# Layer one's gate product on split operands, and eight key pages moved into the second layer's gate

## The reference

```
h = x
layer 0:  h = h + gla_mixer(rms_norm(h, g_pre[0]))            # in-projection q, k, v, g, gated linear attention, w_out
          h = h + sigmoid(rms_norm(h, g_ple[0]) @ w_ple_gate[0]) * (p[0] @ w_ple_up[0])
shared:   k, v = rms_norm(h, g_kv) @ w_kv                      # joined to the paged cache for the samples
layer 1:  h = h + sb_mixer(rms_norm(h, g_pre[1]))              # q and gate from sb_w_in, stick-breaking attention, sb_w_out
          h = h + sigmoid(rms_norm(h, g_ple[1]) @ w_ple_gate[1]) * (p[1] @ w_ple_up[1])
y = rms_norm(h, g_final)
```

## Time and profile before

| | us |
|---|---|
| median of 3 runs | 890.15 (889.59 to 891.01) |
| the profiled execution, its own time | 891.36 |
| its span in the profile | 889.6 |
| PE busy | 846.0 (95%) |
| VectorE busy | 553.7 (62%) |
| ScalarE busy | 455.4 (51%) |
| GpSimd busy | 277.4 (31%) |
| chain that ended last | PE 75%, DVE 10%, DMA 6%, ACT 5% |

### The profile page before, as it was taken

One profiled execution on the slowest core, in us unless ns is written; L12 is line 12 of the kernel. 1 busy time (PEld: TensorE's weight loads), 2 busy tenths in 40 slices (PEclk: granted clock), 3 DMA queues, 4 the chain that ended last, 5 costly groups with the idle time before them and its releaser, 6 DMA issues.

```text
span 889.6 us, 14838 instructions
## 1 busy us (share of the span) xinstructions
PE 846.0 (95%) x5063; PEld 583.9 (66%) x5063; DVE 553.7 (62%) x678; ACT 455.4 (51%) x1532; POOL 277.4 (31%) x151
## 2 busy tenths in 40 slices
PE   5999999989999999999998999999989999999995
PEld 3566677767754444444477878778744444799995
DVE  4345475788856869989996632232267777555553
ACT  4512383237658677769672412212288666444433
POOL 2000000866666998995780000000100000021110
PEclk9999999999999999999999999999999999999998
DMA  9899868646599998989995079998898879321202
GB/s 332 293 398 336 313 234 292 219 151 228 204 308 370 377 331 296 343 311 337 354 339 199 1 248 328 368 332 288 304 339 299 316 269 364 102 95 49 95 1 96
DMA packets 109435, 232.62 MB, mean 261 GB/s; under 512 B 7473, under 2 KB 66488, under 8 KB 109360
## 3 DMA queue, kind: packets, MB, share of 16 engines
q1 hardware_dynamic: 50992, 172.26, 53.2%
q10 hardware_dynamic: 58368, 59.41, 20.0%
HBM read 220.51 MB, written 11.14 MB: 260 GB/s over the span
## 4 chain that ended last, share of the span: by engine, by line
PE 75%; DVE 10%; DMA 6%; ACT 5%; issue 3%; POOL 1%; SPq 1%; ACTq 0%; POOLq 0%; DVEq 0%
PE pp L1652 20%; PE pp L1639 15%; PE pp L1655 10%; PE pp L2087 6%; PE pp L2044 4%; DVE slot L1298 3%; PE pp L2071 2%; PE pp L1616 2%; DMA w_raw<-in_gla_w_in_dram 2%; PE pp L1693 2%; PE pp L2058 2%; PE pp L1636 2%; PE pp L1667 2%; DVE w_lo L1116 1%; DMA slot<-in_cache_k_dram 1%
## 5 line engine op out<-in xcount | busy, mean ns | idle before, releaser
L629 POOL TENSOR_TENSOR slot<-slot,qb 128x1024 f32<-128x1024 f32 x95 | 247.5, 2635 | 100.6 <-DMA slot<-in_cache_k_dram 62.7
L1299 DVE TENSOR_REDUCE zall<-slot 128x16 f32<-128x1024 f32 x99 | 119.0, 1214 | 18.1 <-POOL slot L629 17.0
L1116 DVE TENSOR_TENSOR w_lo<-w_raw,w_hi 128x1024 fp32r<-128x1024 f32 x55 | 77.5, 1408 | 74.5 <-ACT w_hi L674 74.5
L829 ACT ACTIVATE slot<-slot 128x64 f32<-128x64 f32 x464 | 111.0, 241 | 21.8 <-POOL slot L629 21.8
L674 ACT CAST w_hi<-w_raw 128x1024 fp32r<-128x1024 f32 x56 | 58.5, 1045 | 71.3 <-PE pp L1655 34.2
L829 ACT ACTIVATION_READ_ACCUMULATOR slot<-slot 128x1 f32 x464 | 86.8, 187 | 0.0
L1639 PE MATMUL pp<-xn,w_raw 128*128 128x512 f32 x192 | 84.3, 593 | 0.5 <-ACT xn L685 0.5
L1639 PE MATMUL pp<-xn,w_unsplit 128*128 128x512 f32 x192 | 83.9, 592 | 0.0
L1652 PE MATMUL pp<-xb_hi,w_hi 128*128 128x260 f32 x384 | 79.2, 287 | 1.1 <-DVE w_lo L1116 0.9
L1655 PE MATMUL pp<-xa_hi,w_hi 128*128 128x512 f32 x192 | 78.6, 409 | 1.6 <-DVE w_lo L1116 1.6
L1652 PE MATMUL pp<-xb_lo,w_hi 128*128 128x260 f32 x384 | 77.3, 283 | 0.0
(11 more groups left out here) (322 smaller groups left out, 1442.2 us busy)
## 6 DMA issues: line engine op xcount, KB each, us to landing
slot<-in_cache_k_dram SPq DMA_DIRECT2D x128, 512.0 KB, 5.6
slot<-in_cache_v_dram SPq DMA_DIRECT2D x120, 512.0 KB, 5.4
w_raw<-in_gla_w_in_dram ACTq DMA_DIRECT2D x12, 1024.0 KB, 6.2
slot<-in_gla_w_in_dram SPq DMA_DIRECT2D x24, 512.0 KB, 9.5
w_raw<-in_w_kv_dram ACTq DMA_DIRECT2D x8, 1024.0 KB, 9.8
w_raw<-in_w_ple_gate_dram ACTq DMA_DIRECT2D x6, 1024.0 KB, 5.2
s<-in_state_gla_dram SPq DMA_DIRECT2D x1, 4096.0 KB, 19.9
out_dram<-s ACTq DMA_DIRECT2D x4, 1024.0 KB, 8.0
```

Of the source, the lines that this page charges most:

```text
L629: nc.gpsimd.tensor_tensor(slot[s][:], slot[s][:], qb[:, (n // NPG) % 2, :], ALU.mult).then_inc(S("k_mul_pool"), 1)
L829: ins = nc.scalar.activation(part, part, ACT.Copy, accum_out=zall[:, n % NPG, b * SH + h:b * SH + h + 1])
L1116: nc.vector.tensor_tensor(lo, raw, hi.bitcast(F32), ALU.subtract).then_inc(S("w_split"), 1)
L1299: nc.vector.tensor_reduce(zall[:, n % NPG, b * SH:(b + 1) * SH], at.rearrange("p (h d) -> p h d", d=HD), AX.X, ALU.add).then_inc(S("k_used ...
```

## The change

ple0 leaves `UNSPLIT` and becomes a split stage. Its input, set 2 of `X_SETS`, becomes a split set and moves to the B buffers, and VectorE gets an `x_lo` in each job of wo0 (after the page sums in the first six jobs, before them in the last two). The two extra weight buffers now serve only from q1 on (`WHOLE0`): wo0 and ple0 use the two raw ones. In wo0 `load_pair` stands behind ScalarE's `x_hi` of every second job and waits for the products of the pair that used the buffer before. `split_hi` and `split_lo` of ple0's first job stand in wo0's last job (in front of the residual add on VectorE), those of its further jobs at the head of the job before. `PAGES_AT` gives ple0's jobs three pages each, all multiplied by GpSimd, the first summed by ScalarE in every other job; g1's second and third job take four pages each. The turn back of the scores and the sigmoids with the scan move one job later (to g1's sixth job), the turn back of the weights to its eighth.

```diff
@@ -46,13 +46,13 @@
 NJOBS = _j
 WITH_SAMPLES = ("g1", "K", "V", "wo1", "ple1")
 
-UNSPLIT = ("wo0", "ple0", "q1", "g1")
+UNSPLIT = ("wo0", "q1", "g1")
 
 GFINAL, GOUT, BGK, NVEC = 40, 48, 50, 54
 
-X_SETS = ("A", "B", "A", "B", "B", "B", "A")
+X_SETS = ("A", "B", "B", "B", "B", "B", "A")
 X_GAIN = (0, GOUT, 16, 8, 32, None, 24)
-X_SPLIT = (0, 4, 5, 6)
+X_SPLIT = (0, 2, 4, 5, 6)
 
 
 S_STAGES = (("qk", 8), ("v", 8), ("g", 8), ("wo", 8), ("up", 2), ("ple", 8), ("q1", 8))
@@ -65,8 +65,8 @@
 
 
 PAGES_AT = {}
-for _name, _c in (("v", (0, 0, 0, 0, 1, 3, 2, 2)), ("g", (2, 3, 2, 3, 2, 3, 2, 3)), ("wo0", (4,) * 8), ("ple0", (4,) * 8),
-                  ("q1", (4,) * 8), ("g1", (4, 0, 0, 0, 0, 0, 0, 0))):
+for _name, _c in (("v", (0, 0, 0, 0, 1, 3, 2, 2)), ("g", (2, 3, 2, 3, 2, 3, 2, 3)), ("wo0", (4,) * 8), ("ple0", (3,) * 8),
+                  ("q1", (4,) * 8), ("g1", (4, 4, 4, 0, 0, 0, 0, 0))):
     for _u in range(PHASES[_name][1]):
         PAGES_AT[PHASES[_name][0] + _u] = _c[_u]
 PAGES_THROUGH = {}
@@ -93,13 +93,15 @@
 
 QUAD = 4
 
-PAIR_BUF, PAIR_TURN = {}, {}
+WHOLE0 = PHASES["q1"][0] // 2
+PAIR_BUF, PAIR_TURN, PAIR_LAST = {}, {}, {}
 for _p in range(1, NJOBS // 2):
-    _first = PHASES[UNSPLIT[0]][0] // 2
-    _native = _first <= _p < PHASES["K"][0] // 2
-    PAIR_BUF[_p] = (1, 0, 2, 3)[(_p - _first) % 4] if _native else _p % 2
-    PAIR_TURN[_p] = sum(b == PAIR_BUF[_p] for b in PAIR_BUF.values())
-assert PHASES[UNSPLIT[0]][0] // 2 % 2 == 1
+    _four = WHOLE0 <= _p < PHASES["K"][0] // 2
+    PAIR_BUF[_p] = (1, 0, 2, 3)[(_p - WHOLE0) % 4] if _four else _p % 2
+    _before = [_q for _q in range(1, _p) if PAIR_BUF[_q] == PAIR_BUF[_p]]
+    PAIR_TURN[_p] = len(_before) + 1
+    PAIR_LAST[_p] = _before[-1] if _before else None
+assert WHOLE0 % 2 == 1
 
 ZC = 3 * SH
 ZW = NPG * NS // 2 * ZC
@@ -167,8 +169,10 @@
 
 def on_act(n):
 
-    return any(len(pages_at(j)) >= 4 and n in pages_at(j)[:2 if phase_of(j) == "q1" and j % 2 == 0 else 1]
-               for j in PAGES_THROUGH)
+    for j in PAGES_THROUGH:
+        if n in pages_at(j):
+            name, of = phase_of(j), n - pages_at(j)[0]
+            return of < (2 if name == "q1" and j % 2 == 0 else j % 2 if name == "ple0" else len(pages_at(j)) >= 4)
 
 
 def summed_by_act(n):
@@ -330,7 +334,7 @@
         pT0 = at("pT0", [P, 2, NP_TOK], F32, off_small)
         oP = offA + size([P, KT, T])
         pin0 = at("pin0", [P, TB, PLE], F32, oP)
-        xn = {1: at("xn1", [P, KT, T], F32, offA), 2: at("xn2", [P, KT, T], F32, offB), 3: at("xn3", [P, KT, T], F32, oP)}
+        xn = {1: at("xn1", [P, KT, T], F32, offA), 3: at("xn3", [P, KT, T], F32, oP)}
         xb_hi, xb_lo = (at(n, [P, KT, T], F32R, offB + i * size([P, KT, T])) for i, n in enumerate(("xb_hi", "xb_lo")))
 
 
@@ -652,13 +656,14 @@
 
                 if p >= NJOBS // 2:
                     return
-                whole0 = PHASES[UNSPLIT[0]][0] // 2
-                if (unsplit(2 * p) and p >= whole0 + 4) or (p >= 2 and not unsplit(2 * p) and unsplit(2 * p - 4)):
-                    act.wait_ge(S("mm"), tiles_through(2 * (p - 4) + 1))
-                elif PAIR_BUF[p] >= 2:
-                    act.wait_ge(S("mm"), tiles_through(2 * whole0 - 1))
-                elif p >= 3:
-                    act.wait_ge(S("w_split"), splits_through(2 * (p - 2) + 1))
+                q = PAIR_LAST[p]
+                if q is None:
+                    if PAIR_BUF[p] >= 2:
+                        act.wait_ge(S("mm"), tiles_through(2 * WHOLE0 - 1))
+                elif unsplit(2 * q):
+                    act.wait_ge(S("mm"), tiles_through(2 * q + 1))
+                else:
+                    act.wait_ge(S("w_split"), splits_through(2 * q + 1))
                 dst = pair_buffer(p) if unsplit(2 * p) else raw_pair(p)
                 act.dma_start(dst, weight_pair_source(p)).then_inc(S(f"w_in{PAIR_BUF[p]}"), 16)
 
@@ -669,10 +674,11 @@
                 p = j // 2
                 act.wait_ge(S(f"w_in{PAIR_BUF[p]}"), 16 * PAIR_TURN[p])
                 if j >= 4:
-                    act.wait_ge(S("mm"), tiles_through(PHASES["K"][0] - 3 if unsplit(j - 2) else j - 2))
+                    act.wait_ge(S("mm"), tiles_through(j - 2 if not unsplit(j - 2) else
+                                                       PHASES["K"][0] - 3 if phase_of(j) == "K" else PHASES["wo0"][0] - 1))
                 raw, hi, _ = split_views(j)
                 nc.scalar.copy(hi, raw).then_inc(S("w_hi"), 1)
-                if j % 2 == 0 and j > 2 and j != PHASES["K"][0]:
+                if j % 2 == 0 and j > 2 and j not in (PHASES["K"][0], PHASES["ple0"][0]):
                     load_pair(p + 1)
 
             def x_hi(n, src):
@@ -908,17 +914,20 @@
 
             def loads_at(j):
 
-                if j == PHASES["wo0"][0]:
+                if j == PHASES["q1"][0]:
                     load_pair(j // 2 + 2)
                 if j % 2 == 0 and j // 2 + 3 <= PHASES["K"][0] // 2 + 1:
                     load_pair(j // 2 + 3)
 
             for u in range(8):
                 j = PHASES["wo0"][0] + u
-                loads_at(j)
                 sum_page(j)
+                if u == 7:
+                    split_hi(j + 1)
                 act.wait_ge(S("evac"), tiles_through(j))
                 x_hi(2 * KT + u, hT[:, u, 0:NP_TOK])
+                if u % 2:
+                    load_pair(j // 2 + 2)
                 square(KT + u, hT[:, u, 0:NP_TOK])
                 if u == 1:
                     for c in range(2):
@@ -927,7 +936,9 @@
                     rms(1)
             for u in range(8):
                 j = PHASES["ple0"][0] + u
-                loads_at(j)
+                split_hi(j + 1)
+                if u == 7:
+                    load_pair(WHOLE0 + 1)
                 sum_page(j)
                 act.wait_ge(S("evac"), tiles_through(j))
                 sigmoid_tile(8 + u, work[:, 2 + u % 2, 0:NP_TOK], work[:, 2 + u % 2, 0:NP_TOK])
@@ -1013,10 +1024,10 @@
                     if i >= 4:
                         x_hi(4 * KT + 2 * i - 8, hT[:, 2 * i - 8, :])
                         x_hi(4 * KT + 2 * i - 7, hT[:, 2 * i - 7, :])
-                    if i == 4:
+                    if i == 5:
                         for g in range(4):
                             sample_sigmoids(g)
-                    if i == 6:
+                    if i == 7:
                         for g in range(4):
                             sample_weights_out(g)
                 if 8 <= i < 23:
@@ -1408,11 +1419,17 @@
 
             for u in range(8):
                 j = PHASES["wo0"][0] + u
+                if u == 7:
+                    split_lo(j + 1)
                 add_residual(j, u)
-                if u:
+                if u < 6 and u:
+                    score_pages(j)
+                x_lo(2 * KT + u, hT[:, u, 0:NP_TOK])
+                if u >= 6:
                     score_pages(j)
             for u in range(8):
                 j = PHASES["ple0"][0] + u
+                split_lo(j + 1)
                 if u == 0:
                     recip(1)
                 add_gated(j, u, 8 + u, u + 1)
@@ -1462,7 +1479,7 @@
                     sample_rows(done)
                 if i < 8:
                     normed(j, g1T[:, u, :])
-                    if i < 3:
+                    if i < 5:
                         score_pages(j)
                     if i >= 4:
                         x_lo(4 * KT + 2 * i - 8, hT[:, 2 * i - 8, :])
@@ -1642,7 +1659,7 @@
                         last.then_inc(S("mm"), 1)
                     return
                 _, wh, wl = split_views(j)
-                for k in range(KT):
+                for k in tiles:
                     if wait_x:
                         pe.wait_ge(S("x_ready"), x_order(x0 + k) + 1)
                     xh, xl = x_parts(x0 + k)
@@ -1654,7 +1671,8 @@
                         else:
                             last = nc.tensor.matmul(bank[banks_of(j)[0]], w[:, k, :], x[:, 0:NP_TOK],
                                                     start=(k == 0 and first), stop=(k == KT - 1 and w is wl))
-                last.then_inc(S("mm"), 1)
+                if tiles[-1] == KT - 1:
+                    last.then_inc(S("mm"), 1)
 
             def up_tile0(u):
 
```

## The result

The changed kernel took 909.75 us (median of 4, 905.1 to 918.28), the kernel before 889.87 beside it: a ratio of 1.0239 (95% interval 1.0195 to 1.0283). It is slower, as forecast. The size was not: I said 904.1 with 909.0 as the upper end. The profiled execution took 905.1 (span 903.4), 13.7 more than that of before. So the forecast of the sum (+13.95) meets the profiled run, and misses the median by another 4.7.

What follows compares the result with a forecast made beforehand. TensorE, without idle time in wo0's later part and ple0, was taken as the bound. Pair 16 8.05, ple0 0.9, the clock 1.7 and g1 3.3 summed to +13.95 us on 890.15: 904.1, range 894.6 to 909.

Steps and rivals of the forecast that it cites:

- The clock: Start of ple0: one fall to half clock for 3.4 us after the wait for product 36, +1.7 us.
- the first split: End of wo0: job 34's split halves ready at 320.5 to 321.6, covered by the weights' wait, so 0.
- The gain per product: ple0: a product takes 5.68 us split, 6.87 unsplit; 9.5 us over eight, 7.1 from product 36 to q1.
- Pair 16: wo0: weights of jobs 32 and 33 land late with two buffers, at 303.9; product 32 later by 8.05 us.
- The second and third product: ple0's start: products 35 and 36 wait about 4 and 6 us for split weights; +7.5 to 8.5, middle 8.0.
- before product 35 a fall costs nothing, as the next wait absorbs it: ple0's start: a fall to half clock ahead of product 35 adds 0, hidden in the wait for product 36.
- The third rival: Whole kernel: the clock falls twice or more and g1 is at its far end of 6 us: 909; chance 0.14.
- q1: Stage q1: same pages and same products as before, so 0.
- g1: g1 to K: scan a job later, K's first product waits for its split weights; +3.3 us, ends 0 and 6.
- The sum: Whole kernel: 8.05 + 0.9 + 1.7 + 3.3 = +13.95 us, giving 904.1.

Runs made afterwards that it cites:

- second profile: The changed kernel once more, no edit, with a second trace: median 909.98 us, ratio 1.0245; the profiled run took 908.07.
- buffers only: The kernel before with only two raw weight buffers in wo0 and ple0, loads placed as in the change, ple0 unsplit: 906.07 us, ratio 1.0196.
- the last experiment: The changed kernel with the page plan of before and each pair asked for ahead of wo0's page sum: 903.87 us, ratio 1.0195.
- the fillers: Matmuls that nothing reads, put before products 32, 35 and 36 of the changed kernel: 908.02 us, ratio 1.0194.
- pages only: The kernel before with only the change's page plan and later turns and sigmoids: 895.45 us, ratio 1.0051.

## Why the prediction was right in sign and short in size

Two terms of the sum failed. The clock was put at 1.7 us with one fall, where the two profiled runs of the changed kernel show four and five falls that cost 5.4 and nearly 8. And the first split was put at nothing, hidden behind the weights' wait, where product 34 waited a further 1.81 and 3.31 us for it.

- **The gain per product** was right. Jobs 36 to 42 took 50.7 us instead of 56.8, 6.0 less; with the 1.7 us that a fall at 346 cost this is the forecast 7.1 and a little more. TensorE set ple0's period.
- **Pair 16 (+8.05)** was mis-sized and the mechanism right: the load landed in 11.9 us, the wait was 4.79 (4.41 in the second profile). The experiments add what I did not price: when the load goes out. ScalarE's program order decides it, not the product that frees the buffer. They also show that the terms don't add as my sum adds them: the late weights alone (buffers only) cost 16 us of medians, the split on top of them 1.4 more. That the sum meets one profiled run doesn't show what each term is worth by itself.
- **"The first split (hidden)"** failed. With pair 16 late, product 34 still waited 1.81 and 3.31 us for `w_lo`, and 5.52 when it was in time. I had the engines work on while TensorE waited. But ScalarE stood still for 2.66 us before a square, whose buffer TensorE frees with the square sum behind product 33; the page sums, `w_hi` and `w_lo` stand behind that (timelines of ScalarE and VectorE):

```profile
315.93 0.63 ACT L702 ACTIVATE work<-hT 128x512 f32<-128x512 f32 x1 [2.66 <-PE pp L1711]
...
320.29 1.03 ACT L680 CAST w_hi<-w_raw 128x1024 fp32r<-128x1024 f32 x1
```
```profile
321.35 1.45 DVE L1127 TENSOR_TENSOR w_lo<-w_raw,w_hi 128x1024 fp32r<-128x1024 f32 x1 [0.60 <-ACT w_hi L680]
```

So the late job 32 pushed the split back and did not hide it: `w_lo` was ready at 322.8, and I had 320.5 to 321.6. VectorE had been busy until 320.75 and would hardly have begun sooner. Its eight `x_lo` were to be 0.7 us each and to fall in its waits; one took 0.74, the others 1.43 and more beside GpSimd:

```profile
309.45 1.59 DVE L1136 SCALAR_TENSOR_TENSOR xb_lo<-hT,gcol,xb_hi 128x512 fp32r<-128x512 f32 x1
...
313.30 2.81 DVE L1136 SCALAR_TENSOR_TENSOR xb_lo<-hT,gcol,xb_hi 128x512 fp32r<-128x512 f32 x1 [1.66 <-ACT xb_hi L691]
```

- **The second and third product (+7.5 to 8.5)** came at +8.5 in the profiled run and at +11.4 in the second profile. The waits are the other way round from what I had (4 us, then 6): 5.13 and 3.09, since product 35 ran at half clock and took 2.5 us of the second wait. That term is the larger part of the split's price, as the last experiment bears out.
- **The clock (+1.7)** is the term that fell shortest. I had one fall of 3.4 us. There were four in the profiled run, 17.0 us, and 23.8 in the second profile. Three of the four slowed work that no later wait absorbs (job 32's 8.83 less 7.03 is 1.8, which job 34's wait doesn't absorb since its `w_lo` hangs on TensorE's square sums; 1.7 at 346; 1.9 behind K): 5.4 us, and not 1.7. And "before product 35 a fall costs nothing, as the next wait absorbs it" overlooked product 34: a fall there moves the square sum on which job 35's halves wait, 3 us. With it the falls of the second profile cost nearly 8 (1.8, 2.9, 1.7, and 1.3 behind K). From run to run the mean clock goes with the time: 0.985 for 905.1 us, 0.983 and 0.982 for 909.99 and 909.51, 0.973 for 918.28. The 0.012 between first and last is 10.9 us of a span of 910, of 13.2. That the clock is the cause there is not shown: those runs have no trace, longer waits would lower the mean as well, and the fillers lifted it for 2 us of time. The third rival (the clock falls twice or more, 909, to which I gave 0.14) is what came about as to the clock; that its 909 lies so near is luck, as it had g1 at 6 us, which came at 2.9, and the clock at 3.4.
- **q1 (0)** was right: 56.7 us in both. **g1 (+3.3)** was right: +2.9, with a wait of 3.14 for `w_lo_k`, and pages only gives 5.3 us of medians, the fall behind it included.
- **The sum** met the profiled run by luck, since the terms that were too high (pair 16, by 3.3) and the head start of 2.3 stand against those too low (the first split 1.8, the clock 3.7). The range ended at what its third rival gave; it should have allowed for that rival on top of the forecast's own terms.

## What to carry to other kernels

Where a transfer's buffer comes free, look at what stands in the issuing engine's program between that moment and the issue: here the sums of one page (5.5 us for pair 16) and loads of the next stage placed alike turned a saving of memory that costs 3 us into one that costs 16. A cheaper product is worth nothing at a stage's start if the engines that must prepare it run behind TensorE; price that by the first three jobs, not by the period. Where several waits of a few us stand close together, a forecast must allow for a fall of the clock at each, and for the chain that hangs on a product slowed by it.
